# Reordering the opening of a two-block network on one core: x first, root ahead of the modulation sums

## The reference, cut to what matters

```
cond = silu(c)                                        # one row of 1024
mod  = cond @ ada_w + ada_b                           # 6 x 1024: shift1, scale1, gate1, ...
u    = x * rsqrt(mean(x*x) + eps) * norm_mix * (1 + scale1) + shift1
p    = u @ w_in                                       # queries, keys, values, gates
```

## Time and profile before

| | us |
|---|---|
| runs: lowest, median, highest | 949.28, 950.30, 952.63 |
| profiled execution, first to last instruction (span) | 949.0 |
| PE busy in it | 916.4 (97%) |
| DVE busy | 598.6 (63%) |
| ACT busy | 498.1 (52%) |
| POOL busy | 691.2 (73%) |

### The profile page before, as it was taken

The page is one execution under the profiler, slowest core; times in us unless marked ns, Lnnn a source line. Parts: engine busy times, 40 slices in busy tenths (PEclk is TensorE's granted clock), DMA queues, the critical chain, the costliest instruction groups (busy, mean ns, idle before and its releaser), DMA issues.

```text
span 949.0 us, 21725 instructions
## 1 busy us (share of the span) xinstructions
PE 916.4 (97%) x7684; PEld 896.8 (94%) x7684; DVE 598.6 (63%) x1122; ACT 498.1 (52%) x820; POOL 691.2 (73%) x898
## 2 busy tenths in 40 slices
PE   5998999999999999999999999999999999999996
PEld 5887999999999999999999999999989999999996
DVE  3889889767776444523566567774366566877522
ACT  3555655575567665555554455445455444544451
POOL 1786587687769877887676758888857667788873
PEclk9999999999999999999999999999999999999998
DMA  9976567654545557554544435655525444455521
GB/s 360 417 300 238 223 225 272 258 185 171 178 175 182 188 211 260 200 190 177 179 155 156 177 133 187 212 183 208 188 89 179 152 158 159 155 213 186 202 86 45
DMA packets 28225, 185.22 MB, mean 195 GB/s; under 512 B 3027, under 2 KB 5504, under 8 KB 6272
## 3 DMA queue, kind: packets, MB, share of 16 engines
q1 hardware_dynamic: 25832, 167.93, 48.9%
q10 hardware_dynamic: 2328, 16.40, 4.8%
HBM read 183.26 MB, written 1.07 MB: 194 GB/s over the span
## 4 chain that ended last, share of the span: by engine, by line
PE 86%; DVE 8%; issue 2%; ACT 2%; DMA 1%; SPq 0%; POOL 0%; ACTq 0%; POOLq 0%; DVEq 0%
PE mm L609 25%; PE mm L611 25%; PE mm L610 25%; PE mm L643 1%; ACT w_hi L1109 1%; DVE ada_raw L1563 1%; DVE w_lo L1525 1%; DVE score L1683 1%; PE ps_o L991 1%; PE ps_s L974 1%; DMA hot<-onehot 1%; PE ps_o L1065 1%; PE mm L627 1%; PE mm L628 1%; PE mm L629 1%
## 5 line engine op out<-in xcount | busy, mean ns | idle before, releaser
L526 POOL TENSOR_TENSOR w_lo<-raw,w_hi 128x256 fp32r<-128x256 f32 x880 | 680.9, 808 | 235.3 <-ACT w_hi L1109 235.2
L609 PE MATMUL mm<-u_hi,w_hi 128*128 128x256 f32 x1568 | 447.2, 285 | 0.5 <-ACT w_hi L1109 0.3
L610 PE MATMUL mm<-u_lo,w_hi 128*128 128x256 f32 x1568 | 435.7, 278 | 0.0
L611 PE MATMUL mm<-u_hi,w_lo 128*128 128x256 f32 x1568 | 435.5, 278 | 0.0
L1109 ACT ACTIVATE w_hi<-raw 128x1024 fp32r<-128x1024 f32 x291 | 307.6, 1058 | 160.0 <-PE mm L611 150.0
L609 PEld LDWEIGHTS mm<-u_hi,w_hi 128*128 128x128 f32 x1568 | 295.7, 189 | 5.8 <-issue 4.9
L610 PEld LDWEIGHTS mm<-u_lo,w_hi 128*128 128x128 f32 x1568 | 295.8, 189 | 2.0 <-issue 1.9
L611 PEld LDWEIGHTS mm<-u_hi,w_lo 128*128 128x128 f32 x1568 | 295.9, 189 | 0.0
L1525 DVE TENSOR_TENSOR w_lo<-raw,w_hi 128x1024 fp32r<-128x1024 f32 x71 | 95.6, 1346 | 64.3 <-ACT w_hi L1109 54.4
L609 PE MATMUL mm<-h_hi,w_hi 128*128 128x256 f32 x256 | 70.8, 277 | 0.0
L610 PE MATMUL mm<-h_lo,w_hi 128*128 128x256 f32 x256 | 70.7, 276 | 0.0
(11 more groups left out here) (350 smaller groups left out, 1323.8 us busy)
## 6 DMA issues: line engine op xcount, KB each, us to landing
raw<-weights SPq DMA_DIRECT2D x145, 1024.0 KB, 4.8
ada_raw<-ada ACTq DMA_DIRECT2D x14, 1024.0 KB, 5.4
ada_raw<-ada SPq DMA_DIRECT2D x6, 1024.0 KB, 9.5
ada_more<-ada SPq DMA_DIRECT2D x4, 1024.0 KB, 12.1
bias<-tab_scratch SPq DMA_DIRECT2D x1, 1536.0 KB, 9.4
dec<-decay ACTq DMA_DIRECT2D x1, 1536.0 KB, 7.0
x<-xT SPq DMA_DIRECT2D x1, 1024.0 KB, 10.7
out<-x SPq DMA_DIRECT2D x4, 256.0 KB, 2.3
```

What stands on the lines that cost most here:

```text
L526: ins = nc.gpsimd.tensor_tensor(lo[:, at], r[:, at], hi[:, at], ALU.subtract)
L609: nc.tensor.matmul(dst, wh, rhs_hi(k), start=a, stop=False)
L610: nc.tensor.matmul(dst, wh, rhs_lo(k), start=False, stop=False)
L611: i = nc.tensor.matmul(dst, wl, rhs_hi(k), start=False, stop=b)
```

## The change

SP issues `x` first and the small table ahead of the first modulation piece; weight pairs 0 and 1 each move up by one place against the modulation pieces, pair 2 by two. ACT squares `x` before anything else and takes the root before it rounds the first weights. DVE makes variance and diagonals before its first `ada_step`, and then goes chunk by chunk: two `ada_step`, one `first_t`. The remainders of chunks 0 and 1 move from DVE to POOL (`POOL_LO`), and that of weight unit 4 from POOL to DVE. PE has 8 fillers ahead of the sums of squares in place of 36, 16 behind them in place of 7, none behind the spread in place of 8, and new ones ahead of four steps: 34, 8, 12 and 6. `FIRST_ORDER` takes chunk 5 later and chunk 7 of units 0 to 5 last, as before.

```diff
-POOL_LO = [4, 5, 6]
+POOL_LO = [0, 1, 4, 5, 6]
...
+    FIRST_HIGH = {0: 2, 2: 3, 3: 4, 4: 5, 6: 6, 7: 7}
...
-    FIRST_ORDER += [(3, k) for k in range(4)] + [(q, k) for k in (4, 5) for q in range(4)] + [(4, k) for k in range(6)]
-    FIRST_ORDER += [(q, 6) for q in range(5)] + [(5, k) for k in range(7)] + [(q, 7) for q in range(6)]
+    FIRST_ORDER += [(3, k) for k in range(4)] + [(q, 4) for q in range(4)] + [(4, k) for k in range(5)]
+    FIRST_ORDER += [(q, 5) for q in range(5)] + [(5, k) for k in range(6)]
+    FIRST_ORDER += [(q, k) for k in (6, 7) for q in range(6)]
+    WARM_AHEAD = {(0, 0): 34, (0, 1): 8, (0, 2): 12, (0, 3): 6}
...
     def _(sp):
+        sp.dma_start(x[:, :, :], xT).then_inc(S["x_in"], 16)
         sp.dma_start(c_b[:, :], bass.AP(c_row.tensor, 0, [[0, P], [1, D]])).then_inc(S["c_in"], 16)
...
-        ada_load(sp, 0)
         sp.dma_start(ident[:, :], ident_d).then_inc(S["ident_in"], 16)
         sp.dma_start(relb_s[:, :], relb).then_inc(S["tab_in"], 16)
         sp.dma_start(hot[:, :], onehot).then_inc(S["tab_in"], 16)
+        ada_load(sp, 0)
         ada_load(sp, 1)
-        sp.dma_start(x[:, :, :], xT).then_inc(S["x_in"], 16)
+        load(None, 0)
         ada_load(sp, 2)
-        load(None, 0)
+        load(None, 1)
...
         for c in range(12):
-            if c not in (4, 5):
+            if c != 4:
                 low(None, c)
+            if c < 2:
+                row_low(c)
...
         pe.wait_ge(S["ident_in"], 16)
-        keep_warm(36, 0)
+        keep_warm(8, 0)
...
-        keep_warm(WARM[2], 0)
+        keep_warm(16, 0)
         spread(0)
-        keep_warm(8, 0)
...
                 for q, k in FIRST_ORDER:
+                    keep_warm(WARM_AHEAD.get((q, k), 0), 3)
                     first_step(q, k)
...
+        act.wait_ge(S["x_in"], 16)
+        for half in range(2):
+            A(x_sq[:, 4 * half:4 * half + 4, :], x[:, 4 * half:4 * half + 4, :], ACT.Square).then_inc(S["x_squared"], 1)
         act.wait_ge(S["c_in"], 16)
...
+        root(0)
         high(None, 0)
-        root(0)
         high(None, 1)
...
         dve.wait_ge(S["row_ready"], 2)
-        for a in range(6):
-            ada_step(a)
-        variance_in(0)
-        ada_step(6)
-        variance_out(0)
-        ada_step(7)
-        dve.wait_ge(S["rstd_ready"], 1)
-        first_t(0)
...
+        variance(0)
+        for k in range(KC):
             ada_step(2 * k)
             if k == 4:
-                first_t(k)
-            first_lo(k - 1)
-            if k > 4:
-                first_t(k)
+                first_lo(3)
             ada_step(2 * k + 1)
+            if k == 0:
+                dve.wait_ge(S["rstd_ready"], 1)
+            first_t(k)
+            if k == 2:
+                first_lo(2)
+            if k == 4:
+                low(None, 4)
         first_lo(KC - 1)
```

More of the change, by code:

```diff
@@ L70 @@
 PE_TILES = []
-POOL_LO = [4, 5, 6]
-CHUNK_WARM = [0, 0, 0, 0, 5, 5, 5]
+POOL_LO = [0, 1, 4, 5, 6]
 WARM = (6, 5, 7, 2, 10)
@@ L459, in load @@
                 sp.wait_ge(S["lo_pool"], lin(g, 8, n))
+                if p == 6:
+                    sp.wait_ge(S["lo_dve"], 5)
                 if n % 4 == 0 and p > 5:
@@ L469, in _ @@
         sp.dma_start(hot[:, :], onehot).then_inc(S["tab_in"], 16)
+        ada_load(sp, 0)
         ada_load(sp, 1)
-        sp.dma_start(x[:, :, :], xT).then_inc(S["x_in"], 16)
+        load(None, 0)
         ada_load(sp, 2)
-        load(None, 0)
+        load(None, 1)
         ada_load(sp, 3)
-        load(None, 1)
         ada_load(sp, 4)
+        load(None, 2)
         ada_load(sp, 5)
         ada_load(sp, 6)
-        load(None, 2)
         ada_load(sp, 7)
@@ L527, in low @@
             if last == 3:
-                ins.then_inc(S["lo_pool"], 2 if c > 4 and c % 4 == 2 else 1)
+                ins.then_inc(S["lo_pool"], 2 if c == 5 or c > 4 and c % 4 == 2 else 1)
         own = Chain(pool, S["pool_own"])
@@ L556, in _ @@
         for c in range(12):
-            if c not in (4, 5):
+            if c != 4:
                 low(None, c)
+            if c < 2:
+                row_low(c)
             if c == 3:
[L560 to L566, removed]
+                row_low(4)
+            if c == 5:
+                row_low(5)
+                row_low(6)
             if c == 6:
@@ L580, in low_ready @@
         def low_ready(g, c, per_c=8):
-            if g is None and c in (3, 4):
+            if g is None and c == 3:
                 pe.wait_ge(S["lo_pool"], c + 1)
+            elif g is None and c == 4:
+                pe.wait_ge(S["lo_dve"], 5)
             else:
@@ L1130, in _ @@
         act.dma_start(tab_d, tab_s[:, :]).then_inc(S["tab_out"], 16)
-        act.wait_ge(S["x_in"], 16)
-        for half in range(2):
-            A(x_sq[:, 4 * half:4 * half + 4, :], x[:, 4 * half:4 * half + 4, :], ACT.Square).then_inc(S["x_squared"], 1)
+        root(0)
         high(None, 0)
-        root(0)
         high(None, 1)
@@ L1139, in _ @@
             act.wait_ge(S["t_ready"], k + 1)
[L1140 to L1143, removed]
+            ada_read(act, 2 * k + 1)
             if k in POOL_LO:
@@ L1148, in _ @@
                 A(u_hi[:, k, :], t_u[:, k % 2, :], ACT.Identity, bias=mod[:, SHIFT1, k:k + 1]).then_inc(S["uhi_ready"], 1)
-            if 1 <= k < 7:
-                high(None, k + 1)
+            if k in FIRST_HIGH:
+                high(None, FIRST_HIGH[k])
         def take(c, dst, w=P):
@@ L1517, in low @@
         def low(g, c):
-            if c % 4 != 3 or c >= UNITS:
+            if (c % 4 != 3 and (g is not None or c != 4)) or c >= UNITS:
                 return
@@ L1525, in low @@
             V.tensor_tensor(lo, r, hi.bitcast(F32), ALU.subtract)\
-                .then_inc(S["lo_dve"], 8 if g is None and c == 7 else 4)
+                .then_inc(S["lo_dve"], {4: 5, 7: 3}.get(c, 4) if g is None else 4)
         for half in range(2):
```

## The result

The changed kernel took 955.94 us (median of 13 runs; the kernel before 950.44, 13 runs). The ratio, from which one run of 1552.52 us at a mean clock of 0.56 is left out, is 1.0084, 95% interval 1.005 to 1.0118. In a second measurement of the same two kernels (e5) it was 1.0043 (1.0008 to 1.0077). So it is slower, by 4 to 8 us, which is under 1%.

The account below looks back on a forecast made before the run. PE's in-order list, fillers included, was taken to bound the opening: its terms summed to unit 6 at 55.6 against 51.17, 4.4 us later, carried whole to 954.7 us; the 8-in-10 range was 950.7 to 957.9.

Parts of the forecast that it names:

- sums of squares: PE in the opening, behind 8 fillers: 3.5 us at the row's own level, to 18.7; 7.0 at the slow level.
- I carry the whole delay to the end: Behind the opening: DVE's waits there hang on PE's units, so all 4.4 us reach the end of the span.
- table's matmul starts: PE's wait for the small table in the opening: kept at 10.1 us; ends 2.5 us sooner or 0.5 later.
- 16 fillers: PE between sums and spread: 5.4 us, partly at half speed, to 24.1; ends 3.6 all fast, 7.4 all slow.
- 34 fillers: PE between spread and first step: 7.7 us, to 32.4, of which 5 us stand bare.
- first step to unit 6: PE's last part of the opening: 26 fillers, 5.9 us, and 48 steps, 17.3 us, to 55.6.
- rival 2: Opening: sums of squares run at half speed, 7.0 for 3.5 us, chain and list 3.5 later, 958.2 us; chance 0.12.
- The cover: End of opening: DVE's last remainder at 50.0, PE comes to chunk 7 at 53.4, so DVE's chain is covered by 3.4 us.
- the price of a filler: PE's opening: a filler is two instructions, 0.46 us at 1.2 GHz and 0.226 us at 2.4 GHz.
- Rival 1: Opening set by DVE's chain, fillers only fill waits: 1.0 us later, 951.3 us; chance 0.12.
- rival 3: Behind the opening, 46 to 58.5 us: DVE gives PE's delay back, 1.3 us carried, 951.6 us; chance 0.08.
- rival 4: Opening faster: table lands 4.4 us sooner, root early, fillers hidden, 946.9 us; chance 0.06.

Follow-up runs that it names:

- e5: Changed kernel again, unaltered, against the kernel before; 958.52 us (12 runs), ratio 1.0043.
- e13: Changed kernel with 9 and 13 in place of 5 and 7 fillers ahead of and behind the spread of each later norm; 955.32 us, ratio 1.0023.
- e2: Kernel before, its order kept, with the changed kernel's filler counts; 961.33 us, ratio 1.0089.
- e4: Changed kernel without the 60 fillers ahead of the first steps (34, 8, 12, 6); 959.4 us, ratio 1.0059.
- e3: Changed kernel with 20 more fillers ahead of the small table's matmul, where PE waits for the table; 955.24 us, ratio 1.0023.
- e8: e3's kernel with 14 in place of 34 fillers ahead of the first step; 960.34 us, ratio 1.0055.
- e12: Kernel before with 9 and 13 in place of 5 and 7 fillers around the spread of each later norm; 952.48 us, ratio 1.0001.
- e10: e7's kernel, sums of squares ahead of the table, with 25 in place of 16 early fillers; 948.51 us, ratio 0.9978.
- e11: e10's kernel, unit 4's remainder back on POOL, e13's norm fillers, 24, 8, 8, 4 fillers ahead of the steps; 948.65 us, ratio 0.9967.
- e7: Changed kernel, sums ahead of table behind 16 early fillers, root earlier on ACT, 4 fillers before spread, 28 for 34, old step order; 950.73 us, ratio 0.9966.

## Why the prediction was wrong

The forecast was 954.7, with 957.9 as its upper end; by the first ratio the changed kernel stands at 958.3 of 950.3. The direction was right, and in the profiled executions it is PE's list that sets the end. Two terms failed. The sums of squares, put at 3.5 us, took 6.7 in every profile of the changed kernel. And behind the opening, where the text says "I carry the whole delay to the end" and adds nothing, 3 of 12 runs have the late stretch, 8.5 us in the profile. The second is what takes the ratio past the range: the nine runs without it have a mean of 956.4 us (median 955.56) against 950.5 before, which is 956.1 of 950.3. The opening of the profile after, step by step:

| step | forecast us | measured us |
|---|---|---|
| table's matmul starts | 10.1 | 8.98 |
| its matmul, to the first filler | 1.4 | 1.4 |
| 8 fillers | 3.7 | 3.6 |
| **sums of squares** | **3.5** | **6.7** |
| 16 fillers | 5.4 | 6.2 |
| spread | 0.65 | 0.4 |
| 34 fillers | 7.7 | 7.5 |
| first step to unit 6 | 23.2 | 22.8 |
| unit 6 | 55.6 | 57.49 |

- **The step that failed in the opening** is "Sums of squares, 3.5 us ... At the slow level they would take 7.0; I take the row's own level." They took 6.7 in all four profiles and in e13, 6.8 in e2; 3.6 in e4, behind the same 8 fillers. That was rival 2, given 0.12. The text had itself noted that 5.1 us of table and fillers ahead of the sums left no margin, and then took the fast level all the same. In the kernel before 36 fillers stood there, and the sums had the whole rise behind them. The sums' own price is 3.2 us, and the 16 fillers behind them took 0.8 more than forecast. That unit 6 is only 1.9 us later than forecast is luck: the table came 1.1 sooner, and the other rows give 1.0. With the clock up from the table on (e3), unit 6 stands at 51.07.
- By the Trainium skill's TensorE: Matmul & The Clock Gate (Part 1) the point of the rise varies by half a microsecond from run to run. It varies here too, but by more: behind 8 fillers the sums took 6.7 or 6.8 us in six profiles, so it came behind them, and 3.6 in one, where it came ahead of them.
- **The cover was not 3.4 us.** "It is covered by 3.4 us" looked at the last remainder and missed that unit 5 waits for the last product, with 18 steps behind it in the new order and 13 in the old. Its sum also adds the remainders of chunks 2 and 3 and of unit 4 behind the products, while on DVE's list they stand ahead of the last one. The real cover was 0.4 us (the profile after; e8 shows the wait). It didn't change the number, since list and chain were late together, but it is why taking fillers out (e4, e8) gives nothing back.
- **The table** came 1.1 us sooner than the 10.1 kept, inside the bound of 2.5. `hot` still landed behind `x`.
- **Right:** the price of a filler (68 instructions in 7.5 us, 0.22 each two); fillers that stand on the list (in e2 PE has no wait from spread to unit 6, and 60 fillers and 48 steps take 30.7 us, by the prediction's prices 30.9); diagonals done ahead of the spread (DVE had them by 22.2, the spread stood at 26.79 behind 32 filler instructions); no idle PE; the opening's delay carried to the end (6.3 us of 6.5 in e13). Rival 1 falls with e2, rival 3 with e13, rival 4 with the profile.
- **The step that failed behind the opening:** nothing was added there, and the late stretch costs 7 to 8.5 us by the four profiles that have it, and 3 of 12 runs have it (one by its profile, two by time and mean clock). It isn't made by the change's own work: the kernel before has runs of that kind too, and with fillers at the norm neither kernel has any (e12, e13). It lifts the first ratio, since none of the 13 runs of before in that measurement had it. That the change shifts its share is possible and was not settled.

What the ordinary runs' sums did stays open, since no profile caught such a run of the changed kernel. The record suggests that in most of them the opening was shorter than in the profiles: seven of the nine have spans of 951.7 to 954.1 us, while the earliest unit 6 of the four profiles (57.30) and the least time that any profile shows from unit 6 to the end (896.9, e10) make 954.2, an estimate. If their sums ran at 2.4 GHz, as in e4's profile, the forecast of 954.7 was theirs, and the failed step of the opening holds for the other executions alone.

## What to carry to other kernels

Fillers belong where the engine waits anyway: moved behind the data they are paid as far as no other chain is later (in e2 the stretch from spread to unit 6 grew by 7.5 us for 11.8 us of added fillers; in e8 taking 4.5 us out gave nothing), and put ahead of a transfer that is awaited they cost nothing and bring the clock up in time (e3 against the change: 40 instructions more, 6.4 us less in the opening). Where the rows show the array's rise right ahead of a stretch, with no margin, price the stretch at both levels, and take the slow one for as likely as the fast. For the cover of a chain look at every wait on it, banks that are held included, not only at the last one.

## What the runs showed of the hardware

- The granted-clock column reads 1.00 up to its first change, also over fillers and sums that run at 1.2 GHz by their spacing (0.23 and 0.21 us in place of 0.11).
- A fall late in a program can last: PE was busy for all of the 17 us from 705.1 to 722.1 and stood at 1.2 GHz, in units with sums of one column in between. The last such sum was at 717.80.
- With one short fall behind the opening the rest of the program takes nearly the same time whatever the opening: from unit 6 to the end 897.8 us before, 897.2 in e2, 897.7 in e13, 898.0 in e12, 896.9 in e10, 898.2 in e11; e7 is off, with 899.4. With longer or more falls near 70 to 100 us it was 901.5 (e3) and 901.7 (e4), and with the late stretch 905.1 to 908.5.
